# An eleventh buffer for expert weights, with less DMA scratch and a one-column block of ones

## What is computed

```python
for layer in range(DEPTH):                       # DEPTH = 2
    xn = rmsnorm(h, mixer_norm[layer])
    if layer < N_A_LAYERS:                       # layer 0
        mix = retention(xn, ret_w_in[layer], ret_w_out[layer])
    else:                                        # layer 1
        k_sh, v_sh = shared_kv(h, kv_norm, w_kv, k_norm)
        mix = dilated_attention(xn, k_sh, v_sh, dil_wq[j], q_norm[j], dil_wo[j], rel_bias)
    h = h + mix
    hn = rmsnorm(h, ffn_norm[layer]).reshape(B * S, D)
    h = h + hier_moe(hn, router_grp[layer], ..., exp_gate[layer], exp_up[layer], exp_down[layer])
# hier_moe, for each expert e:  (silu(x @ w_gate[e]) * (x @ w_up[e])) @ w_down[e]
```

## Time and profile before

| | |
|---|---|
| median of 3 runs | 1400.0 us (1399.36 to 1400.34) |
| span of the profiled execution, first to last instruction | 1398.8 us |
| PE busy | 1075.8 us, 77% of the span |
| DVE busy | 439.9 us, 31% |
| ACT busy | 343.5 us, 25% |
| moved by DMA | 489.02 MB, mean 350 GB/s |

### The profile page before, as it was taken

The page is one execution under the profiler, slowest core; times in us unless marked ns, Lnnn a source line. Parts: engine busy times, 40 slices in busy tenths (PEclk is TensorE's granted clock), DMA queues, the critical chain, the costliest instruction groups (busy, mean ns, idle before and its releaser), DMA issues.

```text
span 1398.8 us, 15978 instructions
## 1 busy us (share of the span) xinstructions
PE 1075.8 (77%) x6816; PEld 624.8 (45%) x6816; DVE 439.9 (31%) x863; ACT 343.5 (25%) x563; POOL 65.2 (5%) x120
## 2 busy tenths in 40 slices
PE   8999999666547666587999999999666646666586
PEld 8887885222212122132788877775222212122131
DVE  6845526010100101002876666736010100101001
ACT  4334524100001000011655555534100001000010
POOL 2000000000000000000300016300000000000000
PEclk9999999878888788899999999999988879788889
DMA  9655589999999999999755547699999999999997
GB/s 340 237 180 181 221 339 348 427 427 427 429 427 428 427 427 428 427 424 399 220 186 180 180 153 165 169 378 414 430 427 427 428 428 427 427 429 427 428 422 295
DMA packets 75785, 489.02 MB, mean 350 GB/s; under 512 B 6112, under 2 KB 6320, under 8 KB 51136
## 3 DMA queue, kind: packets, MB, share of 16 engines
q1 hardware_dynamic: 71296, 480.53, 84.6%
q0 software_dynamic: 4000, 7.36, 2.8%
q10 hardware_dynamic: 416, 0.07, 0.0%
HBM read 486.77 MB, written 1.17 MB: 349 GB/s over the span
## 4 chain that ended last, share of the span: by engine, by line
DMA 46%; PE 45%; DVE 3%; ACT 2%; issue 1%; SPq 1%; POOL 0%; DVEq 0%; ACTq 0%
DMA ring<-in_exp_up 11%; PE quad L1414 9%; DMA ring<-in_exp_gate 9%; PE quad L380 8%; PE quad L382 8%; PE quad L381 8%; DMA ring<-in_exp_down 6%; PE quad L1433 5%; DMA ring_more<-in_exp_down 5%; DMA ring_rows<-in_exp_up 4%; DMA ring_more<-in_exp_up 2%; DMA ring_rows<-in_exp_gate 2%; DMA ring_more<-in_exp_gate 2%; DMA ring_rows<-in_exp_down 2%; DMA ring<-in_ret_w_in 2%; PE bank L1323 1%
## 5 line engine op out<-in xcount | busy, mean ns | idle before, releaser
L1414 PE MATMUL quad<-ring,work 128*32 128x512 f32 x1136 | 246.3, 704 | 100.1 <-DMA ring_rows<-in_exp_up 24.9
L1414 PE MATMUL quad<-ring_more,work 128*32 128x512 f32 x512 | 186.8, 710 | 57.8 <-DMA ring<-in_exp_up 31.3
L1433 PE MATMUL quad<-ring,work 128*32 128x512 f32 x576 | 138.4, 723 | 57.4 <-DMA ring<-in_exp_down 21.8
L1566 DVE TENSOR_TENSOR work<-work,quad 128x512 f32<-128x512 f32 x16 | 11.0, 688 | 495.7 <-PE quad L1414 437.8
L1433 PE MATMUL quad<-ring_more,work 128*32 128x512 f32 x336 | 115.0, 706 | 58.9 <-DMA ring<-in_exp_down 58.0
L1414 PEld LDWEIGHTS quad<-ring,work 128*32 128x32 f32 x1136 | 61.0, 126 | 196.9 <-issue 186.9
L1575 DVE TENSOR_TENSOR h<-h,bank 128x512 f32<-128x512 f32 x64 | 44.0, 688 | 264.8 <-PE bank L1484 264.8
L1414 PEld LDWEIGHTS quad<-ring_more,work 128*32 128x32 f32 x512 | 42.7, 127 | 120.6 <-issue 113.0
L1503 ACT ACTIVATE work<-bank,gains 128x128 f32<-128x128 f32 x128 | 37.0, 368 | 227.1 <-PE bank L1323 227.1
L362 DVE TENSOR_TENSOR lo_b<-ring,hi_b 128x2048 fp32r<-128x2048 f32 (+1 forms) x40 | 86.2, 2181 | 15.9 <-ACT hi_b L356 15.9
L1433 PEld LDWEIGHTS quad<-ring,work 128*32 128x32 f32 x576 | 33.8, 130 | 108.5 <-issue 105.5
(11 more groups left out here) (341 smaller groups left out, 1825.1 us busy)
## 6 DMA issues: line engine op xcount, KB each, us to landing
ring<-in_exp_gate SPq DMA_DIRECT2D x39, 2048.0 KB, 29.2
ring<-in_exp_up SPq DMA_DIRECT2D x39, 2048.0 KB, 29.2
ring<-in_exp_down SPq DMA_DIRECT2D x34, 2048.0 KB, 28.4
ring_more<-in_exp_gate SPq DMA_DIRECT2D x20, 2048.0 KB, 27.7
ring_more<-in_exp_down SPq DMA_DIRECT2D x19, 2048.0 KB, 28.0
ring_more<-in_exp_up SPq DMA_DIRECT2D x18, 2048.0 KB, 29.2
ring<-in_w_kv SPq DMA_DIRECT2D x12, 2048.0 KB, 8.7
ring<-in_ret_w_in SPq DMA_DIRECT2D x11, 2048.0 KB, 8.8
```

Source lines behind the costliest of these rows:

```text
L1414: last = nc.tensor.matmul(bank[2 + kind][rows, :], m_x[:, k, rows], w[e][:, kk * FF:(kk + 1) * FF], start=(k == 0), stop=(k == KD - 1))
L1433: last = nc.tensor.matmul(bank[4 + nh][rows, :], m_hidT[:, k * P + e * SLOTS:k * P + (e + 1) * SLOTS], w[e][:, at:at + 512], start=(k == 0 ...
L1566: V.tensor_tensor(m_hid[0:M, :], m_sg[0:M, :], bank[3][0:M, :], ALU.mult).then_inc(s["hid_ready"], 1)
```

## The change

`RING` becomes 11. The eleventh buffer, `ring_extra` (slot 10), is memory that no other stage uses, 16 KB per partition. It is paid for by the DMA scratch, whose size is now given as 2048 bytes per partition, and by the block of ones: one column of ones is kept, and `ones` is that column read 128 times (`to_broadcast`).

Slot 10 takes expert tile 0 of each layer, and its request stands among those of the dense tiles: after tile 5 of dense A, and after tile 8 of dense B (`EXTRA_AFTER`). All other first requests keep their buffers and their waits, and each now brings the tile one further on. The end of experts 0 has an order of its own (`MOE_LAST`), so that buffers 2, 3 and 4, which dense B needs first, are not in use at the end. A semaphore of its own (`s_rot`) is dropped in favour of one that exists (`s_fine[1]`).

```diff
-RING = 10
+RING = 11
-MOE_ORDER = ((6, 9, 7, 0, 1, 5, 2, 4, 3, 8), (6, 5, 4, 1, 7, 8, 2, 0, 3, 9))
-AHEAD = 1
+MOE_ORDER = ((10, 6, 9, 7, 0, 1, 5, 2, 4, 3, 8), (10, 6, 5, 4, 1, 7, 8, 2, 0, 3, 9))
+MOE_LAST = (10, 6, 9, 7, 0, 1, 5, 8)
+AHEAD = 2
+EXTRA_SLOT = 10
+EXTRA_AFTER = (5, 8)
...
-    c[:, C_ONES:C_ONES + P] = 1.0
+    c[:, C_ONES] = 1.0
...
-        sb("arena", [P, FULL_RING * TILE + 4 * TT * D + WORK])
+        sb("arena", [P, FULL_RING * TILE + 4 * TT * D + WORK + TILE])
...
+        ring_extra = place("ring_extra", EXTRA_AT, [P, TILE])
...
-        ones = kept[:, C_ONES:C_ONES + P]
+        ones = kept[:, C_ONES:C_ONES + 1].to_broadcast([P, P])
...
+            if n < FIRST_QKV - len(MOE_LAST):
+                return MOE_ORDER[0][(n - FIRST_MOE[0]) % RING]
             if n < FIRST_QKV:
-                return MOE_ORDER[0][(n - FIRST_MOE[0]) % RING]
+                return MOE_LAST[n - FIRST_QKV]
...
+        def moe_extra_sp(sp, layer):
+
+            if layer == 1:
+                sp.wait_ge(s_used, last_tile_in(EXTRA_SLOT, FIRST_QKV) + 1)
+            moe_load(sp, layer, 0)
...
             for n in range(RING, TILES):
-                sp.wait_ge(s_used, first + n - RING + 1)
-                load(n)
+                sp.wait_ge(s_used, last_tile_in(slots_in_order[first + n], first + n) + 1)
+                moe_load(sp, layer, n)
...
             for i in range(1, N_WIN):
                 load_tile(sp, FIRST_WIN + i, win[:, :, i * COLS:(i + 1) * COLS], KD)
+                if i == EXTRA_AFTER[0]:
+                    moe_extra_sp(sp, 0)
...
                 load_tile(sp, FIRST_QKV + i, src, KD)
+                if i == EXTRA_AFTER[1]:
+                    moe_extra_sp(sp, 1)
...
-    nc = _bacc.Bacc("TRN2", target_bir_lowering=False, num_devices=1)
+    nc = _bacc.Bacc("TRN2", target_bir_lowering=False, num_devices=1, dynamic_dma_scratch_size=2048)
```

More of the change, by code:

```diff
@@ L95 @@
 C_TRI = C_IDENT + P
-C_ONES = C_TRI + P
-C_IOTA = C_ONES + P
-C_KEPT = C_IOTA + P
+C_IOTA = C_TRI + P
+C_ONES = C_IOTA + P
+C_KEPT = C_ONES + 1
 C_COS = C_KEPT
@@ L184, in build @@
         WORK_AT = H_AT + TT * D
+        EXTRA_AT = WORK_AT + WORK
         def place(name, word, shape, dt=F32):
@@ L268, in slot @@
                 return ring_rows[:, :]
+            if at == EXTRA_SLOT:
+                return ring_extra[:, :]
             return ring[:, at, :] if at < FULL_RING else ring_more[:, at - FULL_RING, :]
@@ L521, in scaled_rotation_dve @@
         def scaled_rotation_dve(dve, chain):
-            dve.wait_ge(s_rot, 16)
+            dve.wait_ge(s_fine[1], 16)
             dve.wait_ge(t_step, ROW_SPREAD)
@@ L1017, in by_rows, with moe_load @@
             return (it, kind) == (0, 0)
+        def moe_load(sp, layer, n):
+            first = FIRST_MOE[layer]
+            rows = moe_rows(layer)
+            it, j = n // MOE_TILES, n % MOE_TILES
+            kind = ("gate", "up", "down")[j // PER_GROUP]
+            at = slots_in_order[first + n]
+            if by_rows(it, j // PER_GROUP):
+                sp.dma_start(slot(at).rearrange("p (e c) -> p e c", e=PER_GROUP),
+                             rows["gate"][:, 0:PER_GROUP, 2 * j * FF:2 * (j + 1) * FF]).then_inc(s_ring[at], 16)
+                return
+            if by_pairs(it, j // PER_GROUP):
+                e = it * PER_GROUP + j % 2 * 2
+                half = (j - PER_GROUP) // 2
+                sp.dma_start(slot(at).rearrange("p (e c) -> p e c", e=2),
+                             rows["up"][:, e:e + 2, half * KD // 2 * FF:(half + 1) * KD // 2 * FF]
+                             ).then_inc(s_ring[at], 16)
+                return
+            if not by_halves(it, j // PER_GROUP):
+                e = it * PER_GROUP + j % PER_GROUP
+                sp.dma_start(slot(at).rearrange("p (e c) -> p e c", e=1),
+                             rows[kind][:, e:e + 1, :]).then_inc(s_ring[at], 16)
+                return
+            here = slice(it * PER_GROUP, (it + 1) * PER_GROUP)
+            part = j - 2 * PER_GROUP
+            if part < 2:
+                e = it * PER_GROUP + 2 * part
+                sp.dma_start(slot(at).rearrange("p (e c) -> p e c", e=2),
+                             rows["down"][:, e:e + 2, 0:2 * D]).then_inc(s_ring[at], 16)
+                return
+            dst = slot(at).rearrange("p (e k c) -> p e k c", e=PER_GROUP, k=2)
+            for k, landed in enumerate((s_fine[part - 2], s_ring[at])):
+                sp.dma_start(dst[:, :, k, :], last_down[layer][:, here, 2 + k, (part - 2) * 512:(part - 1) * 512]
+                             ).then_inc(landed, 16)
@@ L1057, in moe_sp @@
             if ahead:
                 sp.wait_ge(r_o_done, 2 * RET_H)
-                for n in range(AHEAD):
-                    load(n)
+                for n in range(1, AHEAD):
+                    moe_load(sp, layer, n)
                 return
-            for n in range(AHEAD if layer == 0 else 0, RING):
+            for n in range(AHEAD if layer == 0 else 1, RING):
                 at = slots_in_order[first + n]
@@ L1447, in last_down_half @@
                 n = first + it * MOE_TILES + 2 * PER_GROUP + 2 + nh
-                pe.wait_ge(s_fine[nh], 16 * (layer + 2 - nh))
+                pe.wait_ge(s_fine[nh], 16 * (layer + 2))
                 at = slot(slots_in_order[n])
@@ L2195, in _ @@
             sp.dma_start(first[:, KD // 2:KD, :], win[:, KD // 2:KD, 0:COLS]).then_inc(s_ring[0], 16)
-            sp.dma_start(work[:, 16384:16384 + 2 * S], constants[:, C_COS:C_COS + 2 * S]).then_inc(s_rot, 16)
+            sp.dma_start(work[:, 16384:16384 + 2 * S], constants[:, C_COS:C_COS + 2 * S]).then_inc(s_fine[1], 16)
             for i in range(1, N_WIN):
                 load_tile(sp, FIRST_WIN + i, win[:, :, i * COLS:(i + 1) * COLS], KD)
+                if i == EXTRA_AFTER[0]:
+                    moe_extra_sp(sp, 0)
             moe_sp(sp, 0, True)
```

35 lines of the change are left out of this document (1 added, 34 removed).

## The result

The changed kernel takes 1388.27 us (median of 4 runs, 1387.66 to 1389.12) against 1399.68 us of the kernel before beside it (4 runs, 1398.64 to 1400.34): a ratio of 0.992, 95% interval 0.9907 to 0.9932, so 11.4 us less. The profiled execution has a span of 1385.9 us at a granted clock of 0.901.

The account below looks back on a forecast made before the run. Expert stages were taken as bound by the weight stream, dense stages by PE. Two tiles of 4.92 us, all other terms 0: 1400.0 - 9.84 = 1390.2 us, range 1387.5 to 1394.5.

Parts of the forecast that it names:

- -4.92 us in each layer: Expert stages: with tile 0 loaded in the dense stage, 85 tiles are left instead of 86, saving 4.92 us each.
- The sign named for it: Experts 0: the first last-up tile that PE waits for was to land at 276.4 instead of 281.35 us.
- the transfer was hidden anyway: Rival, gap before 226 us: the stream just idles 4.9 us longer, no gain, 1400.0 us; chance 0.03.
- one gain is lost: Rival, dense B or a stage's start: thin cover costs as much as one tile, 1395.1 us; chance 0.06.
- Depth gives nothing: Expert stages: the stream is already full with ten buffers, so a deeper queue was taken as 0.
- The passage into dense B: End of experts 0: `dil_wq` moves with the last expert tile; new buffer order has 20 us cover, cost 0.
- The extra loads for nothing: Dense A and B: two extra loads of 4.92 us of stream each cost 0, bounds 0 to 1 us.
- The column of ones: Weight loads from a repeated column take 0.19 us as from the block, cost 0; if twice as long, 3.0 us.
- The scratch: POOL's DMA requests: with an eighth of the room, POOL waits only where nobody wants the data soon, cost 0.
- a gain at the start is at most 0.7 us: First 40 us: smaller constants gain at most 0.7 us; a loss was bounded by the same 0.7.
- The rival on POOL: Attention: each request takes c longer, costing 42 c - 10.8 us; at c = 0.75, 1410.9 us; chance 0.06.

Follow-up runs that it names:

- e1: Changed kernel with both early requests taken out, slot 10 first requested once PE has used the layer's first tile: 1398.29 us, ratio 0.9988 to the kernel before.
- e5: Changed kernel with the early request kept in layer 0 only; layer 1's waits for PE's first use: 1394.25 us, ratio 0.9957 to the kernel before.
- e6: Changed kernel with both extra tiles requested behind the dense stage's last weights, ahead of the ten others: 1389.36 us, ratio 0.9926 to the kernel before.
- e8: Changed kernel run again without an edit, as reference: 1388.78 us, ratio 0.9923 to the kernel before.
- e2: Kernel before with only the DMA scratch set to 2048 bytes per partition: 1398.12 us, ratio 0.9988.
- e10: Changed kernel with layer 0's extra tile requested behind dense tile 1 instead of tile 5: 1394.34 us, ratio 0.9961 to the kernel before.
- e4: Kernel before with only the block of ones replaced by one column read 128 times: 1399.83 us, ratio 0.9999.
- e3: Kernel before, default scratch, with layer 0's router loads held until PE has used two dense tiles: 1398.99 us, ratio 0.9991.
- e11: Kernel before with layer 1's router weights loaded in dense B instead of amid experts 0: 1397.39 us, ratio 0.9982.
- e7: Changed kernel with layer 1's router weights loaded in dense B, after the last query tile: 1386.14 us, ratio 0.9904 to the kernel before.
- e9: Changed kernel with 1280 instead of 2048 bytes of DMA scratch: 1389.95 us, ratio 0.9931 to the kernel before.

## Why the prediction was right

It gave 1390.2 us (1387.5 to 1394.5); the time was 1388.3. Point by point:

- **-4.92 us in each layer: right, and shown.** e1 takes both away and loses 9.5 to 10.0 us, for a sum of 9.84; e5 takes one away and loses 5.5; what is left over e1 is 4.0. The reason given, that a tile carried before the first reuse leaves one tile less to a full stream, is what e6 shows too: the tile goes into idle time of the stream, and the time is kept. The sign named for it, layer 0's first awaited up tile at 276.4 us, came at 275.10 (275.82 in e8); the difference is about the 1.07 us of the start. The rivals that the transfer was hidden anyway and that one gain is lost fall with e1 and e5.
- **Depth gives nothing: right.** e1 against e2: 1398.3 and 1398.1 us, at 427 GB/s in both. (The text read 427 to 430 GB/s in 11 slices of each expert stage; the earlier trace rows has ten, and one at 424 and 422. Nothing hangs on it.)
- **The passage into dense B: right.** All that came before is passed on: `dil_wq` is requested at 638.92 instead of 644.84, 5.92 us, of which 4.92 were forecast and the rest is the start.
- **The extra loads for nothing: right.** No DMA wait stands behind tile 5 or tile 8. e10 shows what the missing cover would have cost.
- **The column of ones: right** (e4).
- **The scratch: 0 was the term that was off.** The text said that a gain at the start is at most 0.7 us, from the constants, and counted POOL's pauses there only as harmless. The small scratch is a gain: 1.07 us at the first reuse in the trace of the changed kernel, and 1.9 us by e2's medians. The traces say that the pauses hold POOL's router loads back from a full stream that PE waits for; e3 left this unproved. With it, 9.84 + 1.07 = 10.9 us of the 11.1 to 11.4 measured. That the forecast came within 1.9 us of the measurement rests on the two tiles; this term was missed, and its size is near the noise.
- **The rival on POOL: its mechanism does not exist in that form.** It priced a longer request, each time.
In the two profiled executions the ends are 12.9 us apart, more than the medians. The first of the 16 DMA engines to finish the last tile does so 10.9 us earlier (1385.2 and 1374.3 us); the last one 13.1 us earlier, since in the trace of before one engine was 6.1 us behind the first, and in that of after 3.9. This spread belongs to the execution: in e4, whose requests are those of before, it is 4.2 us, and over all the traces 3.6 to 6.1. That the 10.9 us meet the sum above to the tenth is luck too: against the trace of e1 (1384.7) it is 10.4 us, and with that of e8 (1375.0) in place of after 9.7. In e2 that first engine is only 0.2 us earlier than in before, so the start's 1.07 us cannot be followed to the end in single traces.

## What to carry to other kernels

Where a saturated stream bounds a stage, as here, a further buffer is worth one tile's transfer, and only if its first request is made before the first buffer would come free anyway: count tiles moved into idle time of the stream, not depth. Small requests in a full stream count too: read the GB/s of each stretch beside its busy share, and move what nobody waits for to where the stream is idle. And before you place a transfer for free, find the cover; in front of a waiting PE, in e10, it cost its own length and the clock on top.

## What the hardware showed that I had not expected

- **Small requests cost far more than their bytes.** Router weights of layer 1, four requests of POOL of 162 KB together (0.4 us at 427 GB/s), took the stream from 427 to 393 GB/s over 20 us at a busy share of 1.00, and cost 2.5 us in e11 and 2.6 us in e7.
- **A scratch too small for the requests in flight was a gain here,** 1.9 us by e2's medians: POOL pauses for 3.2 to 9.0 us, and its requests are spread out. With 1280 bytes a pause came on the path, and DVE waited 2.7 us (e9).
- **An idle PE can lose its clock:** in e10 PE had no work for 3.7 us at the start; the granted clock went from 1.00 to 0.50 (2.4 to 1.2 GHz), stayed there until about 45 us, and so cost 2.9 us on top of the idle time. In e3, with 2.65 us idle, its mean was 0.83 from 20 to 30 us. The same idle time does not always do it: after 1.86 us without work ahead of 9.9 us the granted clock was 0.50 from 12 to 14 us in the trace of before, and after 1.89 us at the same place it was 1.00 in that of after.
- **A landing is as late as the slowest of 16 engines.** In experts 1 of the trace after, the 16 parts of a tile ended within 1.9 us at 1018 us and within 3.6 us at 1323 us; in that of before it was 3.2 us at 1015 and 4.8 us at 1325. The landing for which PE waits, 1369.26 us in before, is that of the last part; the first was 4.8 us ahead.
